# Weight slots with offsets of their own, inner tiles 2064 bytes apart, and h on a 2048-byte boundary: a two-layer float32 decoder on one core

## The reference

```
# first layer
h = rms_norm(x, norm1_w);   proj = h @ w_in                  # 2048 -> 10792 columns
o_nsa, o_dn = sparse_attention(proj), gated_deltanet(proj)
mixed = g_nsa * (o_nsa @ w_up_nsa) + g_dn * (o_dn @ w_up_dn)
x = x + mixed @ w_o
h2 = rms_norm(x, norm2_w)
x = x + (silu(h2 @ w_ffn_gate) * (h2 @ w_ffn_up)) @ w_ffn_down   # 5632 inner channels
# second layer: the same frame with w_in_2, an RWKV mixer and latent attention, w_out_2,
# and a feed-forward with a three-tap convolution on its gate; then a last rms_norm
```

## Time and profile before

| | |
|---|---|
| time of two runs | 2855.41 and 2857.13 us, median 2856.27 |
| profiled execution, first to last instruction (span) | 2854.1 us; no time of its own is listed beside the span |
| mean granted clock of TensorE | 0.996 of full speed |
| busy: TensorE, its weight loads, VectorE, ScalarE, GpSimd | 98%, 85%, 72%, 48%, 17% of the span |
| read from HBM | 469.80 MB, 165 GB/s over the span |

### The profile page before, as it was taken

The page is one execution under the profiler, slowest core; times in us unless marked ns, Lnnn a source line. Parts: engine busy times, 40 slices in busy tenths (PEclk is TensorE's granted clock), DMA queues, the critical chain, the costliest instruction groups (busy, mean ns, idle before and its releaser), DMA issues.

```text
span 2854.1 us, 41789 instructions
## 1 busy us (share of the span) xinstructions
PE 2791.8 (98%) x16404; PEld 2428.2 (85%) x16404; DVE 2051.3 (72%) x3158; ACT 1363.8 (48%) x2043; POOL 479.0 (17%) x526
## 2 busy tenths in 40 slices
PE   8999999999999999999999999999989999999998
PEld 7888888888888888888888888878778888888887
DVE  7987787766766666656657889878777777667655
ACT  6453455455554544444446545434354444434434
POOL 2111011110111111001002734511021111001101
PEclk9999999999999999999999999999999999999999
DMA  6444334455555555555556433321445555555555
GB/s 227 163 156 162 112 124 131 144 190 187 192 186 191 187 190 190 188 190 192 188 179 212 162 112 128 101 67 52 148 146 187 191 187 190 191 190 188 192 177 162
DMA packets 132243, 474.63 MB, mean 166 GB/s; under 512 B 14672, under 2 KB 14928, under 8 KB 131792
## 3 DMA queue, kind: packets, MB, share of 16 engines
q1 hardware_dynamic: 132048, 471.96, 50.0%
HBM read 469.80 MB, written 2.10 MB: 165 GB/s over the span
## 4 chain that ended last, share of the span: by engine, by line
PE 89%; DVE 5%; ACT 3%; POOL 1%; issue 1%; DMA 0%; SPq 0%; DVEq 0%; ACTq 0%; POOLq 0%
PE ps L893 88%; DVE ringl L1859 1%; DVE U L1859 1%; ACT high L1399 1%; POOL U L2540 1%; DVE xT L1859 1%; PE ps L896 1%; ACT hr L1399 0%; ACT U L1399 0%; POOL U L2613 0%; DVE U L1868 0%; ACT U L1412 0%; DMA xT<-in_x_dram 0%; DVE hx L1859 0%; DVE U L2056 0%
## 5 line engine op out<-in xcount | busy, mean ns | idle before, releaser
L893 PE MATMUL ps<-hr,high 128*128 128x512 f32 x4672 | 1508.0, 401 | 19.4 <-DVE ringl L1859 17.2
L1859 DVE TENSOR_TENSOR ringl<-ring,high 128x1024 fp32r<-128x1024 f32 x880 | 1080.5, 1230 | 424.5 <-ACT high L1399 423.8
L1399 ACT ACTIVATE high<-ring 128x1024 fp32r<-128x1024 f32 x880 | 914.4, 1041 | 635.8 <-PE ps L893 626.5
L893 PEld LDWEIGHTS ps<-hr,ringl 128*128 128x128 f32 x4672 | 880.0, 188 | 205.6 <-issue 1.4
L893 PE MATMUL ps<-hr,ringl 128*128 128x256 f32 x4672 | 920.6, 278 | 0.0
L893 PEld LDWEIGHTS ps<-hr,high 128*128 128x128 f32 x4672 | 721.9, 189 | 29.4 <-issue 15.1
L893 PE MATMUL ps<-yur,high 128*128 128x512 f32 x2176 | 684.3, 395 | 10.2 <-DVE xT L1859 6.7
L2540 POOL TENSOR_TENSOR U<-U,rs 128x256 f32<-128x256 f32 x292 | 263.0, 901 | 1701.3 <-DVE U L1859 1682.0
L893 PEld LDWEIGHTS ps<-yur,ringl 128*128 128x128 f32 x2176 | 409.4, 188 | 90.8
L1399 ACT ACTIVATE U<-ps 128x256 f32<-128x256 f32 (+3 forms) x481 | 172.7, 371 | 601.2 <-PE ps L893 575.6
L893 PE MATMUL ps<-yur,ringl 128*128 128x256 f32 x2176 | 430.3, 279 | 0.0
(11 more groups left out here) (178 smaller groups left out, 1255.0 us busy)
## 6 DMA issues: line engine op xcount, KB each, us to landing
ring<-in_w_dram SPq DMA_DIRECT2D x870, 512.0 KB, 3.3
ring<-in_w_dram SPq DMA_DIRECT2D x32, 256.0 KB, 3.3
xT<-in_x_dram SPq DMA_DIRECT2D x3, 512.0 KB, 8.1
out_dram<-hx SPq DMA_DIRECT2D x3, 512.0 KB, 2.8
cst<-in_cst_dram SPq DMA_DIRECT2D x1, 1374.5 KB, 12.5
yT<-in_lora_dram SPq DMA_DIRECT2D x1, 1024.0 KB, 7.8
xT<-in_x_dram SPq DMA_DIRECT2D x2, 256.0 KB, 4.7
U<-in_lora_dram SPq DMA_DIRECT2D x1, 512.0 KB, 5.8
```

The costliest lines, as they stand in the source:

```text
L893: return e.matmul(out, l, r, start=start, stop=stop)
L1399: return e.activation(out, i, ACT.Copy, scale=scale)
L1859: return e.tensor_tensor(out, a, b, op)
```

## The change

Three things about addresses, and no instruction more or less.

- Slot i of `ring` begins RING_PAD[i] floats later than before in the tensor, that is 0, 16, 32, 64, 128 or 256 bytes; slot i of `high` HIGH_PAD[i] floats later, 0, 16, 64 or 256 bytes. All users take the place from `ring_slot` and `high_slot`.
- An inner tile (high and low part, 2048 bytes) begins 2064 bytes after the one before it.
- The function `onto` moves the next tensor up to a multiple of 2048 bytes: once before `hx`, and once so that the first inner tile, 256 floats into the arena, lies on one.

Modulo 2048, `hx` then begins at 0, the ring slots at 0, 16, 32, 64, 128 and 256, the high slots at 256, 272, 320 and 512, `yT` at 1600, the mix tiles at 0, and inner tile t at 16 t. The arena is 640 floats smaller.

```diff
+RING_PAD = [0, 4, 8, 16, 32, 64]
+HIGH_PAD = [0, 4, 16, 64]
+INNER = 512 + 4
...
+        def onto(n, past=0):
+            while (base + 4 * (place[0] + past)) % n:
+                place[0] += 16
+
+        def ring_slot(m):
+            return (m % RING) * BLK + RING_PAD[m % RING]
+
+        def high_slot(k):
+            return (k % HIGH) * BLK + HIGH_PAD[k % HIGH]
...
         xT_ = sb("xT", 16 * SEQ)
+        onto(2048)
         h_at = place[0]
         hx_ = sb("hx", 32 * SEQ)
         ring_at = place[0]
-        ring = sb("ring", RING * BLK)
-        ringl = sb("ringl", RING * BLK, F32R, at=ring_at)
-        high = sb("high", HIGH * BLK, F32R)
+        ring = sb("ring", RING * BLK + RING_PAD[-1])
+        ringl = sb("ringl", RING * BLK + RING_PAD[-1], F32R, at=ring_at)
+        high = sb("high", HIGH * BLK + HIGH_PAD[-1], F32R)
...
         yT_ = sb("yT", 16 * SEQ)
+        onto(2048, 256)
         u_at = place[0]
...
-        axr = shaped(yur[:, u_at - y_at + 256:u_at - y_at + 256 + 64 * SEQ], 32, 2, SEQ)
+        def inner(ap, at):
+            return shaped(ap[:, at:at + 32 * INNER], 32, INNER)[:, :, 0:512].rearrange("p t (b n) -> p t b n", b=2)
+
+        axr = inner(yur, u_at - y_at + 256)
...
-        ar.at = mark1 + 64 * SEQ
+        ar.at = mark1 + 32 * INNER
...
-                        at = (m % RING) * BLK + off
-                        g = (order[m] % HIGH) * BLK + off if m in order else 0
+                        at = ring_slot(m) + off
+                        g = high_slot(order[m]) + off if m in order else 0
...
-                slot = (m % RING) * BLK
+                slot = ring_slot(m)
```

More of the change, by code:

```diff
@@ L557, in build @@
         hhF, hlF, hh, hl = hx[:, :, 0, :], hx[:, :, 1, :], hxr[:, :, 0, :], hxr[:, :, 1, :]
-        axr = shaped(yur[:, u_at - y_at + 256:u_at - y_at + 256 + 64 * SEQ], 32, 2, SEQ)
+        def inner(ap, at):
+            return shaped(ap[:, at:at + 32 * INNER], 32, INNER)[:, :, 0:512].rearrange("p t (b n) -> p t b n", b=2)
+        axr = inner(yur, u_at - y_at + 256)
         ah, al = axr[:, :, 0, :], axr[:, :, 1, :]
-        alF = shaped(U_[:, 256:256 + 64 * SEQ], 32, 2, SEQ)[:, :, 1, :]
+        alF = inner(U_, 256)[:, :, 1, :]
         flat = shaped(hx_[:, :], 32, SEQ)
@@ L1543, in split @@
                 n = blocks[m][2] * len(blocks[m][3])
-                o, g = (m % RING) * BLK, (k % HIGH) * BLK
+                o, g = ring_slot(m), high_slot(k)
                 e.wait_ge(s_ring[m % RING], 16 * (m // RING + 1))
@@ L1977, in split @@
                 n = blocks[m][2] * len(blocks[m][3])
-                o, g = (m % RING) * BLK, (order[m] % HIGH) * BLK
+                o, g = ring_slot(m), high_slot(order[m])
                 e.wait_ge(hi.sem, hi.after(m))
```

## The result

The changed kernel takes 2873.57 us (2872.42 and 2874.71), the one before 2856.27; the ratio is 1.0063 with a 95% interval of 1.0046 to 1.0080. It is 17.3 us slower, where I had forecast 10 us faster. The time lies in the range of the prediction, and the sign is wrong. The interval reaches 0.17% to either side, so far less than the 2% that I had taken as the limit of the measurement can be told.

What follows compares the result with a forecast made beforehand. TensorE's matmuls were taken as the bound, busy 2791.8 of 2854.1 us. Terms -15.7 (h), +5.6 (inner tiles) and 0 (slots) summed to -10 us, a span of 2844 or 2846 us on the median's scale; range 2804 to 2900.

Steps and rivals of the forecast that it cites:

- loads and splits are covered: Weight loads, ScalarE roundings and VectorE subtractions: any slowing by 16-byte offsets stays hidden behind TensorE, cost 0.
- the bounds of 0.68 to 0.71 us: All weight products: fastest and slowest four (high, high, low, low matmuls) from timeline pieces, -50 or +53 us for everything together.
- The inner stride: Down products, 704 fours: tiles 2064 bytes apart give 0.698 us a four, +5.6 us, between -7 and +14.
- I take zero for the slots: Each weight slot's own offset, touching all 3424 fours: 0 us net.
- part one: Fours with h moving, 2336: h on a 2048-byte boundary takes them from 0.6967 to 0.690 us, -15.7 us.
- the three steady levels: Fours before the change: 0.690 us with mix and inner tiles moving, 0.697 with h, 0.706 in the second up half.
- the phase of the moving operand alone: Fours with h moving: only the moving operand's start modulo 512 bytes sets their speed; basis of the -15.7 us.
- C: Every four: distance to the weights counts and today's is among the better; +39 us, 2895 us, or +53, 2909; chance 0.24.
- the deciding point: Mean four of 0.698 us, from which the slots' offsets eat the gain from moving h and C holds.
- A: Stretches of matmuls: addresses do nothing, something else such as neighbouring matmuls makes the difference; 2856 us, chance 0.16.
- B: Weight and moving-operand reads: 16 and 32 bytes of skew break up locked collisions; 2762 us if half the pool went; chance 0.16.
- Rival D: Odd slots' loads or splits grow by over 2 us, TensorE waits each sixth block; +150 us, chance 0.02.

Runs made afterwards that it cites:

- the sweep: Changed kernel with roomier slots and feed-forward weight offsets swept in one execution: equal for ring and high, 2866.11 us; in a second run unequal, 2862.78 us.
- 128 with 240: High slots 128 and ring slots 240 bytes past moving operands at 0 modulo 256, whole kernel; ratio 1.0053 to the kernel before.
- the trace at 28: All weight slots 28 bytes past moving operands at 0 modulo 256, whole kernel; median 2857.24 us, ratio 1.0019 to the kernel before.
- the three fast ones: Kernel before with only h moved, 2842.41 us; that with second-half y also at 192, 2841.35; changed kernel with all slots at 1472, no offsets, 2846.42.

## Why the prediction was wrong

**What was right.** TensorE's matmuls are all that counts, loads and splits are covered, and the place of the operands in memory makes the difference between 0.690, 0.697 and 0.706 us. All of that held, and the levels after the change lie inside the bounds of 0.68 to 0.71 us for a mean four. As bounds of what any place can give they were too narrow: the sweep found 0.740 us at 108. The inner stride was forecast at +5.6 us and cost 6.8 alone.

**The step that failed** is "I take zero for the slots". Alone they cost 14.7 us, and inside the change they also undo part one: the slots' places were 27 us of it. The reason that I gave for zero was that the three steady levels lie on both sides of any average I could form, and beside it stood their plain mean, 0.698 us, 3 ns above the kernel's own 0.6946. Drawing many places means getting the mean of all places; the sweeps put that at 0.700 us. The honest value of the term was 3424 x (0.698 - 0.6946) = +12 us from the rows that I had, which with the other two terms makes +2 us and just turns the sign. For the inner tiles I had taken such a mean, and it held; for the slots I didn't.

**Part one** was nearly right for h alone (-15.7 forecast, -13.0 measured) and was wrong in the change, where the fours with h moving became 0.0038 us longer and not 0.007 shorter. I had read the three levels as the phase of the moving operand alone. They allow the distance to the weights as well, since the weights stood at one phase everywhere, so no row could tell the two apart; the run with everything at 0, 2860 us with h on the boundary, did. A term worked out under one of two readings that the rows allow was carried as if it were certain. The prediction announces bounds for the other reading in its sum, and the sum has none.

**The rivals.** C described what happened: the distance counts and the one before was among the better ones. Its place was right (every four), its price too high, +39 us for 0.706 us where the mean came to 0.7007; and the deciding point, a mean four of 0.698 us, was passed. One of its reasons was wrong: a distance of 256 bytes is the same as 0, 0.697 us. A is refuted by the single parts, which move the time by -13.0, +14.7 and +6.8 us with addresses alone. B had the mechanism of a locked pattern half right, but skewing the addresses by 16 or 32 bytes breaks up nothing. Rival D didn't occur: ScalarE waited 8.1 us for loads. C was given 0.24; with rows on both sides and no row for a single new distance it deserved as much as the forecast.

By the rule that TensorE never waits on anyone (the Trainium skill, "SBUF — State Buffer", section "Who interferes with whom") the places of the operands could not have moved the time of any of these twelve kernels. The trace disagrees: fours from 0.687 to 0.740 us with the same instructions at the same clock.

## What to carry to other kernels

Where TensorE is the bound, compare the distance between matmul starts with the columns at the granted clock, stretch by stretch; if the same instructions run at different speeds, the places of the two operands are worth a try, and they cost nothing. Try one fixed distance for all weights and moving tiles, and judge it over whole executions, since a place that is fast over a few blocks may have slower rhythms too. Of the fixed places tried here over whole kernels (0, 28, 108, 192, and 128 with 240) only 192 beat the kernel before, by 0.5%. Offsets that differ from slot to slot give the mean of all places, which is a loss for a kernel that stands on a good one.

## What the runs showed of the hardware that was not expected

The spacing of fp32r matmuls of 256 and 512 columns depends on the start of the stationary operand minus that of the moving one, modulo 256 bytes, and not on where the two lie. One step of 4 bytes can be worth 40 ns in a four of 0.70 us (0.700 at 104 bytes, 0.740 at 108, 0.703 at 112). The levels of a four are mostly 6.7 ns apart, 16 cycles of 2.4 GHz. At one distance several rhythms are possible (0.687, 0.700 and 0.707 us at 28; 0.703 and 0.740 us at 108). In the trace at 28 two unbroken chains of over a thousand fours stayed each in its own, 0.707 and 0.687 us, and four matmuls of the norm were enough to tip it for 730 us. Splitting on ScalarE and VectorE and the loads are not touched by 16-byte offsets. That weight loads and the moving operand's reads collide is the explanation that I assume; what part of the memory makes the pattern wasn't measured. At 192 single fours of 0.70 to 0.71 us do occur beside side work, at most three in a row in the four traces that were taken (the kernel before and the three fast ones). Whether 192 has a slow rhythm that holds, and that the fifteen executions of these three kernels didn't meet, stays open.
